# A depthwise convolution on VectorE: every tap accumulates in PSUM, in two alternating halves of 512 columns

## What is computed

```python
def conv_mixer(u, buf, w_in, conv_w, conv_b, ln_g, ln_b, w_out):
    z = u @ w_in
    a, b, gate = jnp.split(z, 3, axis=-1)
    c = a * jax.nn.sigmoid(b)
    full = jnp.concatenate([buf.astype(c.dtype), c], axis=1)
    y = lax.conv_general_dilated(full, conv_w[:, None, :], window_strides=(1,), padding='VALID',
        dimension_numbers=('NWC', 'WIO', 'NWC'), feature_group_count=D_CONV)
    y = y + conv_b
    y = jax.nn.silu(layer_norm(y, ln_g, ln_b))
    out = (y * jax.nn.silu(gate)) @ w_out
    return out, full[:, -(CONV_WIDTH - 1):]
```

## Time and profile before

| | us |
|---|---|
| median of 3 runs (lowest to highest) | 3276.52 (3274.56 to 3279.51) |
| the profiled execution | 3278.45 |
| its span in the trace | 3276.8 |
| busy: PE / DVE / POOL / ACT | 3075.6 / 1506.5 / 1548.1 / 850.2 |
| tap instructions with the accumulator in SBUF: 224, together | 422.1 |
| tap instructions with the accumulator in PSUM: 240, together | 306.4 |

### The profile page before, as it was taken

One profiled execution on the slowest core, in us unless ns is written; L12 is line 12 of the kernel. 1 busy time (PEld: TensorE's weight loads), 2 busy tenths in 40 slices (PEclk: granted clock), 3 DMA queues, 4 the chain that ended last, 5 costly groups with the idle time before them and its releaser, 6 DMA issues.

```text
span 3276.8 us, 50429 instructions
## 1 busy us (share of the span) xinstructions
PE 3075.6 (94%) x19117; PEld 2962.2 (90%) x19117; DVE 1506.5 (46%) x1729; ACT 850.2 (26%) x1708; POOL 1548.1 (47%) x1153
## 2 busy tenths in 40 slices
PE   6999999999989999999968999999999999899996
PEld 6999999999989999999947899899899889799985
DVE  6999999999931114000082233433443443500043
ACT  5121112211122214122142222322322322422332
POOL 2778778787733333333344233333333323244475
PEclk9999999999999999999989999999999999899998
DMA  5121221212122224222273211211211211432386
GB/s 163 41 71 50 57 60 47 71 50 57 51 92 95 89 96 170 71 65 72 86 253 113 64 48 43 61 45 45 58 42 48 61 39 48 157 95 87 108 290 219
DMA packets 171676, 284.86 MB, mean 87 GB/s; under 512 B 62008, under 2 KB 72504, under 8 KB 171576
## 3 DMA queue, kind: packets, MB, share of 16 engines
q1 hardware_dynamic: 127328, 222.48, 22.2%
q10 hardware_dynamic: 41912, 52.32, 4.4%
q0 software_dynamic: 2352, 8.88, 0.7%
HBM read 218.44 MB, written 67.15 MB: 87 GB/s over the span
## 4 chain that ended last, share of the span: by engine, by line
PE 46%; issue 23%; DVE 16%; ACT 5%; POOL 5%; DMA 3%; ACTq 1%; DVEq 1%; SPq 0%; POOLq 0%
PE z_even L515 8%; PE z_even L516 8%; PE z_even L518 8%; PE z_odd L515 7%; PE z_odd L516 6%; PE z_odd L518 6%; POOL w_lo L1030 3%; DVE aux L1327 3%; DVE work L1327 2%; DMA work<-conv_scratch 2%; ACT work L948 1%; DVE work L1423 1%; POOL work L1139 1%; DVE work L1426 1%; DVE work L1429 1%
## 5 line engine op out<-in xcount | busy, mean ns | idle before, releaser
L1030 POOL TENSOR_TENSOR w_lo<-w_raw,w_hi 128x512 fp32r<-128x512 f32 x528 | 745.2, 1420 | 1364.7 <-ACT w_hi L744 1364.2
L515 PE MATMUL z_even<-u_hi,w_hi 128*128 128x364 f32 (+1 forms) x2784 | 926.8, 333 | 88.9 <-POOL u_lo L1191 33.8
L515 PE MATMUL z_odd<-u_hi,w_hi 128*128 128x364 f32 (+1 forms) x2784 | 939.3, 337 | 58.0 <-POOL w_lo L1030 58.0
L516 PE MATMUL z_even<-u_lo,w_hi 128*128 128x364 f32 (+1 forms) x2784 | 923.0, 332 | 0.0
L516 PE MATMUL z_odd<-u_lo,w_hi 128*128 128x364 f32 (+1 forms) x2784 | 922.8, 331 | 0.0
L744 ACT ACTIVATE w_hi<-w_raw 128x512 fp32r<-128x512 f32 x528 | 331.3, 630 | 1681.7 <-PE z_even L518 804.6
L518 PE MATMUL z_odd<-u_hi,w_lo 128*128 128x364 f32 (+1 forms) x2784 | 636.6, 330 | 0.0
L518 PE MATMUL z_even<-u_hi,w_lo 128*128 128x364 f32 (+1 forms) x2784 | 635.9, 330 | 0.0
L515 PEld LDWEIGHTS z_even<-u_hi,w_hi 128*128 128x128 f32 x2784 | 531.0, 191 | 106.9 <-issue 35.8
L515 PEld LDWEIGHTS z_odd<-u_hi,w_hi 128*128 128x128 f32 x2784 | 531.6, 191 | 96.7 <-POOL w_lo L1030 54.5
L516 PEld LDWEIGHTS z_odd<-u_lo,w_hi 128*128 128x128 f32 x2784 | 532.2, 191 | 0.1
(11 more groups left out here) (149 smaller groups left out, 2174.4 us busy)
## 6 DMA issues: line engine op xcount, KB each, us to landing
w_raw<-in_w SPq DMA_DIRECT2D x528, 256.0 KB, 2.6
work<-in_x SPq DMA_DIRECT2D x32, 544.0 KB, 5.3
work<-branch_scratch SPq DMA_DIRECT2D x31, 544.0 KB, 5.4
conv_scratch<-work ACTq DMA_DIRECT2D x16, 544.0 KB, 2.7
work<-conv_scratch SPq DMA_DIRECT2D x16, 544.0 KB, 3.8
resid_scratch<-work ACTq DMA_DIRECT2D x16, 544.0 KB, 5.6
branch_scratch<-work ACTq DMA_DIRECT2D x16, 512.0 KB, 2.6
branch_scratch<-work POOLq DMA_DIRECT2D x15, 544.0 KB, 3.0
```

The lines of the kernel that those rows point to most:

```text
L515: pe.matmul(o, w_hi[:, q, at:at + P], chunk(u_hi[:, k, :], c), start=(i == 0), stop=False)
L516: pe.matmul(o, w_hi[:, q, at:at + P], chunk(u_lo[:, k, :], c), start=False, stop=False)
L1030: pool.tensor_tensor(w_lo[:, q, :], w_raw[:, q, :], w_hi[:, q, :].bitcast(F32), ALU.subtract).then_inc(w_lo_ready, 1)
```

## The change

All taps accumulate in aux1, and odd_taps is gone, with the instruction that wrote it first and the addition at the end. Each tap is done in two instructions of 512 columns, one for each bank of aux1; they alternate, so each waits, as before, for the instruction two places ahead of it. The two instructions of the last tap raise conv_ready, which ACT now awaits at twice its count.

```diff
-        (r_a, sig, ..., ys, prod, odd_taps) = places(T, T, T, T, T, T, TP + 32, SB * SEG, TS, 4 * SS * CW, TP)
+        (r_a, sig, ..., ys, prod) = places(T, T, T, T, T, T, TP + 32, SB * SEG, TS, 4 * SS * CW)
...
             def read_conv(j):
-                act.wait_ge(conv_ready, j + 1)
+                act.wait_ge(conv_ready, 2 * j + 2)
...
+            TAPS = 2 * (CW - 2)
             def glu(j, nxt):
-                ge(dve, conv_ready, j)
+                ge(dve, conv_ready, 2 * j)
...
                 dve.wait_ge(z_read, 2 * j + 2)
-                dve.tensor_scalar(odd_taps, cp[:, 1:1 + TP], cols[:, bass.ds(C_CW + j * CW + 1, 1)], None,
-                                  ALU.mult).then_inc(tap, 1)
                 dve.wait_ge(tap0_ready, j + 1)
-                for i in range(2, CW):
-                    if i > 2:
-                        dve.wait_ge(tap, (CW - 1) * j + i - 2)
-                    acc = odd_taps if i % 2 else aux1
-                    dve.scalar_tensor_tensor(out=acc, in0=cp[:, i:i + TP],
-                                             scalar=cols[:, bass.ds(C_CW + j * CW + i, 1)], in1=acc,
-                                             op0=ALU.mult, op1=ALU.add).then_inc(tap, 1)
+                for i in range(1, CW):
+                    for h in range(2):
+                        if i > 1:
+                            dve.wait_ge(tap, TAPS * j + 2 * (i - 2) + h + 1)
+                        ins = dve.scalar_tensor_tensor(
+                            out=aux[:, h, :], in0=cp[:, i + 512 * h:i + 512 * h + 512],
+                            scalar=cols[:, bass.ds(C_CW + j * CW + i, 1)], in1=aux[:, h, :],
+                            op0=ALU.mult, op1=ALU.add)
+                        ins.then_inc(tap if i < CW - 1 else conv_ready, 1)
                     if i == CW // 2 and nxt:
                         read_z(2 * j + 2, z_even, sig, r_a)
-                dve.wait_ge(tap, (CW - 1) * j + CW - 1)
-                dve.tensor_tensor(aux1, aux1, odd_taps, ALU.add).then_inc(conv_ready, 1)
```

More of the change, by code:

```diff
@@ L136, in places @@
             return out
-        (r_a, sig, y_st, y_sq, acc_y, acc_y2, cp, cs_flat, ys, prod, odd_taps) = places(
-            T, T, T, T, T, T, TP + 32, SB * SEG, TS, 4 * SS * CW, TP)
+        (r_a, sig, y_st, y_sq, acc_y, acc_y2, cp, cs_flat, ys, prod) = places(
+            T, T, T, T, T, T, TP + 32, SB * SEG, TS, 4 * SS * CW)
         cs = cs_flat.rearrange("p (b s) -> p b s", b=SB)
```

## The result

The changed kernel takes 3220.84 us (median of 4 runs, 3215.82 to 3228.34) against 3277.79 for the kernel before, a ratio of 0.9826 with a 95% interval of 0.9812 to 0.9839. It is 57 us faster. The forecast was 3218 us, with a range of 3208 to 3246.

A forecast was written before the change was run, and what follows sets the result against it. DVE's closed ring of 51.13 us a step was taken to bound the convolution stage; at 45.8 PE's 47.57 bounds, the norm starts 58.7 us earlier, 3278.45 becomes 3219.8, the median 1.9 lower: 3218 us, range 3208 to 3246.

The forecast's parts named there:

- DVE's closed ring: Convolution stage before the change: DVE's self-dependent cycle takes 51.13 us a step, and POOL's work for PE hangs on it.
- SBUF taps are long only beside POOL: DVE taps with SBUF accumulator: 1269 ns at best, 1780 median, 3633 worst; long only where POOL has an instruction running.
- 0.655 us per half tap: DVE's new 512-column PSUM taps: 740 ns long less 86 overlap, 60 of them 39.3 us a step against 44.4 removed.
- The rival of the fixed part showing twice: DVE taps without overlap, 0.740 us apart: ring 50.9 us, nothing gained, 3274 us; chance 0.05.
- The slower rival, the uncovered wait: DVE taps 0.78 us apart, the wait two places ahead uncovered: ring 53.3 us, 3312 us; chance 0.08.
- That rival's ring of 51.07: DVE's present step used to set the tap spacing, 0.743 us, above which the change begins to be slower.
- PE becomes the bound, with little to spare: Convolution stage: DVE's ring falls to 45.8 us, below PE's pair of 47.57, by 1.8 us a step.
- The wait for z_even: DVE mid-step: half the taps done at e + 22.5, PE delivers z_even at e + 23.8, a new 1.3 us wait.
- POOL is late next, by 1.1 us to spare: POOL's w_lo for the odd tile's third quarter: ready at e + 34.6, needed by PE at e + 35.7; no stall counted.
- The case of a partial gain: POOL's third quarter late in many steps: 2 us lost per step, 30 in all, 3248 us; chance 0.12.
- The sum: PE's 16 pairs lose 56.0 us of stalls; the norm starts at 846.2 rather than 904.90, 58.7 us earlier; profiled execution 3219.8.

The follow-up runs named there:

- the eight extra instructions: Changed kernel with 8 more half-tap-form instructions ahead of each step's taps, written to a spare SBUF place: 3287.12 us, ratio 1.0022 against the kernel before.
- the two extra ones: Changed kernel with 2 more half-tap-form instructions ahead of each step's taps, written to a spare SBUF place: 3223.97 us, ratio 0.9823 against the kernel before.
- the order in sequence: Changed kernel with all taps of the first half, then all of the second, each waiting for the one directly ahead: 3367.11 us, ratio 1.0271 against the kernel before.

## Why the prediction was right

*DVE's closed ring, not POOL, sets the step.* This is shown by the eight extra instructions, with which PE waits for short w_lo again, and by the two extra ones, which cost nothing. (In the earlier trace rows DVE's nines fill slices 2 to 11, not 3 to 11 as the prediction has it; it is the same stage.)

*SBUF taps are long only beside POOL.* This is shown by the kernel without the samples' convolution: the same form takes 1276 ns in the median, and 1271 to 1279 wherever POOL runs nothing.

*0.655 us per half tap.* Measured were 0.659: a duration of 751 ns on average (740 worked out), less 92 (86). The rival of the fixed part showing twice falls with it. In the prediction's sentence on the Trainium skill, VectorE: DVE Perf Modes, the advice to have few operations stands in the section Rules for kernel authors, and the section that it names, The DRAIN you can't avoid, goes on to say that a next operation that is not held starts earlier. Starts 0.659 apart at a length of 0.751 are earlier in that sense. The slower rival, the uncovered wait, is real: it is what the order in sequence shows, with a bound (0.78) that is about right on the tap itself (0.79) and too small behind register arithmetic (0.90). The change escapes it by its alternation. (That rival's ring of 51.07 should read 51.13, which moves its limit from 0.743 to 0.744.)

*PE becomes the bound, with little to spare.* This was right: in step 3 the sum ends at 272.26 (252.41 + 19.85), 2.4 us ahead of the odd tile's end at 274.67 (227.09 + 47.58), where 2.7 were worked out. (The 2.9 us that DVE waits there also hold the 0.5 from the tile's end to the first write of cp.) Inside, two terms were off. Taps begin 3.7 us after the odd tile's end (227.09 to 230.78), not 2.8; 0.5 of that is the time from the tile's end to the first write (227.60), which the prediction put at nothing without a reason. The wait for z_even is 0.44 rather than 1.3, and that follows from the first: the time at which PE delivers z_even does not depend on the taps, so taps that begin 0.9 later wait 0.9 less. So the two cancel by the mechanism and not by luck.

*POOL is late next, by 1.1 us to spare.* It has some 8 us: the third quarter's w_lo is begun 26.4 us after the odd tile's end (253.45) and ends at about 27.6, needed at 35.7. The 18.9 us of the samples' convolution were the slow figure, taken as a bound; beside PSUM taps it is 12.3. The case of a partial gain, 0.12 in the forecast, rested on that figure, which the change itself removes.

*The sum.* From the start of tile 2 to the norm 764.0 us are measured (84.37 to 848.38), 763.4 were worked out (82.84 to 846.2). The clock held 1.00 in the stage. The profiled execution took 3228.34 us where 3219.8 were worked out: tile 2 began 1.5 us later, the stage took 0.6 longer, and 6.4 were lost behind the norm. That the median of the runs lies within 3 us of the forecast is partly luck, since the four runs spread over 12.5 us.

## What to carry to other kernels

When a trace names an engine as the releaser of a wait, look for the engine that no longer waits for the bottleneck itself: here VectorE waited for TensorE once in 16 steps, its ring ordered ScalarE's work and through it GpSimd's, and the bottleneck's waits carried GpSimd's name. Here a VectorE tap with one of its two tensor inputs in PSUM was not held up beside a busy GpSimd (745 to 760 ns over 960 taps), and did not hold it up either (w_lo at 1297 ns), so an accumulator that is updated many times can be worth its PSUM banks. And a chain on one accumulator wants a second independent chain in between, above all in a loop, where the wait can sit on register arithmetic ahead of the work (0.90 us a half tap in sequence, 0.659 in alternation).

## What the runs showed of the hardware that was not expected

- A VectorE tap that waits for the one directly ahead begins 0.04 us after its end when the wait is on the tap itself (0.79 apart at 0.755 long on average; 1.325 at 1.289), and 0.14 to 0.15 after it when the wait is on register arithmetic ahead of the tap (0.90 at 0.755; 1.433 at 1.289).
- Halving instructions that are held up beside GpSimd raised their total hold-up per step from 8.5 to 13.3 us.
- GpSimd's w_lo subtraction took 1724 ns on average in the stage beside SBUF taps, and 1297 beside PSUM taps:

```profile
L1030 POOL TENSOR_TENSOR w_lo<-w_raw,w_hi 128x512 fp32r<-128x512 f32 x128 | 165.3, 1297 | 288.0 <-ACT w_hi L744 288.0
```
